# A fused five-part transformer kernel on one core: a new order of steps in a gated delta rule and its output units, and index scores computed by pairs of heads without their causally masked quarter

## What is computed

```python
idx = jnp.einsum('bqhd,bsd->bqhs', iq_c, ik)
score = jnp.einsum('bqhs,bqh->bqs', jax.nn.relu(idx), iw_c)
score = jnp.where(kpos[None, :] <= qpos[:, None], score, -jnp.inf)
sel = lax.top_k(score, k_top)[1]
```

```python
a_strict = jnp.where(strict, jnp.einsum('bhncd,bhnmd->bhncm', k_beta, k) * decay, 0.0)
sol = lax.linalg.triangular_solve(eye + a_strict, rhs, left_side=True, lower=True, unit_diagonal=True)
...
o = rmsnorm(o, out_gain).astype(proj.dtype) * jax.nn.silu(z)
...
x = x + jnp.concatenate([y_gdn, y_sc], axis=-1) @ w_mix_out[l]
```

## Time and profile before

| | us |
|---|---|
| median of 3 runs | 2455.21 |
| lowest and highest | 2454.68, 2456.13 |
| the profiled execution: its time | 2454.87 |
| its span in the trace | 2453.1 |
| TensorE busy | 2406.0 (98%) |
| VectorE busy | 1623.0 (66%) |
| ScalarE busy | 1172.2 (48%) |

### The profile page before, as it was taken

The page is one execution under the profiler, slowest core; times in us unless marked ns, Lnnn a source line. Parts: engine busy times, 40 slices in busy tenths (PEclk is TensorE's granted clock), DMA queues, the critical chain, the costliest instruction groups (busy, mean ns, idle before and its releaser), DMA issues.

```text
span 2453.1 us, 35283 instructions
## 1 busy us (share of the span) xinstructions
PE 2406.0 (98%) x14059; PEld 2075.4 (85%) x14059; DVE 1623.0 (66%) x1978; ACT 1172.2 (48%) x1406; POOL 156.7 (6%) x141
## 2 busy tenths in 40 slices
PE   7999999999999999999999999999999999999998
PEld 6888988888888888888978888888888888888887
DVE  6998886555775777596665445455877467755774
ACT  5434574544464654642554345344554334433433
POOL 1000000000200100000000000000122002200220
PEclk9999999999999999999999999999999999999999
DMA  8555546454425465554065655445565556556554
GB/s 247 190 188 172 172 138 223 140 192 144 153 84 193 146 196 175 177 166 138 3 240 172 200 183 182 155 138 172 172 202 177 204 184 193 187 190 199 178 178 147
DMA packets 337332, 422.42 MB, mean 172 GB/s; under 512 B 8478, under 2 KB 263212, under 8 KB 336700
## 3 DMA queue, kind: packets, MB, share of 16 engines
q1 hardware_dynamic: 334204, 410.87, 51.0%
q0 software_dynamic: 2544, 8.52, 1.1%
q10 hardware_dynamic: 464, 1.32, 0.2%
HBM read 418.53 MB, written 2.10 MB: 171 GB/s over the span
## 4 chain that ended last, share of the span: by engine, by line
PE 91%; DVE 5%; ACT 2%; issue 1%; DMA 0%; POOL 0%; SPq 0%; ACTq 0%; DVEq 0%
PE ps L732 35%; PE ps L733 18%; PE ps L786 10%; PE ps L788 10%; PE ps L787 10%; PE ps L1061 1%; DVE w_lo L2081 1%; ACT w_hi L1354 1%; PE ps L1053 1%; PE ps L735 1%; PE ps L736 1%; PE ps L737 1%; PE ps L979 1%; PE ps L1273 1%; PE ps L1264 1%
## 5 line engine op out<-in xcount | busy, mean ns | idle before, releaser
L732 PE MATMUL ps<-h_cat,w_hi 128*128 128x512 f32 x3840 | 1349.5, 397 | 9.8 <-DVE h_cat L2224 4.5
L733 PE MATMUL ps<-h_cat,w_lo 128*128 128x256 f32 x3840 | 1068.2, 278 | 0.0
L732 PEld LDWEIGHTS ps<-h_cat,w_hi 128*128 128x128 f32 x3840 | 720.5, 188 | 182.7 <-issue 12.2
L733 PEld LDWEIGHTS ps<-h_cat,w_lo 128*128 128x128 f32 x3840 | 722.8, 188 | 2.2 <-issue 1.9
L2081 DVE TENSOR_TENSOR w_lo<-ring,w_hi 128x2048 fp32r<-128x2048 f32 (+2 forms) x279 | 588.3, 2111 | 170.7 <-ACT w_hi L1354 168.1
L1354 ACT ACTIVATE w_hi<-ring 128x2048 fp32r<-128x2048 f32 (+2 forms) x279 | 492.6, 1767 | 94.5 <-PE ps L788 63.1
L2077 DVE TENSOR_TENSOR w_lo<-ring,w_hi 128x2048 fp32r<-128x2048 f32 (+1 forms) x136 | 302.8, 2232 | 231.1 <-ACT w_hi L1351 228.2
L1351 ACT ACTIVATE w_hi<-ring 128x2048 fp32r<-128x2048 f32 (+1 forms) x136 | 252.7, 1862 | 276.1 <-PE ps L788 254.9
L786 PE MATMUL ps<-w_hi,h_cat 128*128 128x512 f32 x640 | 250.5, 391 | 1.8 <-DVE w_lo L2077 1.8
L788 PE MATMUL ps<-w_hi,h_cat 128*128 128x512 f32 x640 | 249.2, 389 | 0.0
L787 PE MATMUL ps<-w_lo,h_cat 128*128 128x512 f32 x640 | 249.0, 389 | 0.0
(11 more groups left out here) (420 smaller groups left out, 2278.7 us busy)
## 6 DMA issues: line engine op xcount, KB each, us to landing
ring<-in_w_ffn_up SPq DMA_DIRECT2D x44, 2048.0 KB, 8.0
ring<-in_w_mix_in SPq DMA_DIRECT2D x28, 2048.0 KB, 8.3
ring<-in_even_w_in SPq DMA_DIRECT2D x27, 2048.0 KB, 8.0
ring<-in_w_ffn_down SPq DMA_DIRECT2D x16, 2048.0 KB, 8.2
ring<-in_odd_w_in SPq DMA_DIRECT2D x11, 2048.0 KB, 8.3
ring<-in_even_w_out SPq DMA_DIRECT2D x8, 2048.0 KB, 8.0
ring<-in_odd_w_out SPq DMA_DIRECT2D x8, 2048.0 KB, 8.0
ring<-in_w_mix_out SPq DMA_DIRECT2D x8, 2048.0 KB, 8.3
```

Source lines behind the costliest of these rows:

```text
L732: mm(o[:, 0:2 * T], whi[slot][:, k, :], flat(cat[:, k]), start=first, stop=False)
L733: ins = mm(o[:, T:2 * T], wlo[slot][:, k, :], cat[:, k, 0, :], start=False, stop=end)
```

## The change

1. Index scores on TensorE go by pairs of heads (2p, 2p+1), and within a pair by the 128 queries: head 2p then head 2p+1 for the first queries against keys 0 to 127 only, then both for the second queries against all 256 keys. Pairs (0, 1), (2), (3, 4), (5), (6, 7) follow units 0 to 4 of `o_gate1`. The relu and the sums work on 384 columns in place of 512; the quarter of `isum` that is now not written is set to zero once (it is masked in any case before the top-k).
2. `log_rows` of c goes ahead of `a_turn` on TensorE, and only `log_rows` of d waits for the last `g_b` tile. `attn` of a and b goes ahead of the last `post` of `g_b` on VectorE.
3. `roots_table`, a square root of one column, stands on ScalarE behind `join2_c` of b.
4. The splits of `g_out`: unit 1 goes ahead of `o_copy` of c on ScalarE and ahead of `o_total(1)` on VectorE; unit 2 goes ahead of the two `h_cat<-qkv` steps on VectorE.

```diff
@@ index scores, TensorE
-            for h in range(3 * j, min(3 * j + 3, IDX_HEADS)):
-                if h >= 6:
-                    pe.wait_ge(sem["relu_ready"], h - 5)
-                r = slice(IDX_DIM * (h % 2), IDX_DIM * (h % 2) + IDX_DIM)
+            for p in ((0, 1), (2,), (3, 4), (5,), (6, 7), (), (), ())[j]:
+                two = (2 * p, 2 * p + 1)
+                if p >= 3:
+                    pe.wait_ge(sem["relu_ready"], two[1] - 5)
                 for qt in range(TT):
-                    ins = mm(ps[2 + h % 6][:, qt * T:(qt + 1) * T], iq[r, h // 2, qt * P:(qt + 1) * P], ik[r, :],
-                             start=True, stop=True)
-                ins.then_inc(sem["idx_ready"], 1)
+                    for h in two:
+                        r = slice(IDX_DIM * (h % 2), IDX_DIM * (h % 2) + IDX_DIM)
+                        keys, c = (qt + 1) * P, qt * P
+                        ins = mm(ps[2 + h % 6][:, c:c + keys], iq[r, p, qt * P:(qt + 1) * P], ik[r, 0:keys],
+                                 start=True, stop=True)
+                        if qt == TT - 1:
+                            ins.then_inc(sem["idx_ready"], 1)
@@ relu, ScalarE
-            af(relu[:, h % 2].rearrange("p a t -> p (a t)"), ps[2 + h % 6][:], ACT.Relu).then_inc(sem["relu_ready"], 1)
+            af(relu[:, h % 2], ps[2 + h % 6][:, 0:P + T], ACT.Relu).then_inc(sem["relu_ready"], 1)
@@ log_rows, TensorE
             if t:
                 after(pe, "attn", 0, 1)
-                pe.wait_ge(sem["posted"], S["g_b"].s0 + 8)
+                if hh:
+                    pe.wait_ge(sem["posted"], S["g_b"].s0 + 8)
@@ ScalarE, the loop over its steps
+        def roots_table():
+            af(sm["sp"][:, 0:1], eps[:], ACT.Sqrt)
...
+            if (name, key) == ("join2_c", (0, 1)):
+                roots_table()
             if (name, key) == ("uw_c", (1, 1)):
                 split_to(S["g_out"].n0 + 1)
-            if (name, key) == ("o_square", (1,)):
+                after(act, "state", 0, 1)
                 split_to(S["g_out"].n0 + 2)
@@ VectorE, the loop over its steps
+        for hh in range(2):
+            go("attn", 0, hh)
...
-            if (name, key) == ("o_total", (1,)):
+            if (name, key) == ("o_gate", (0,)):
                 split_to(S["g_out"].n0 + 2)
+        split_to(S["g_out"].n0 + 3)
         for q in range(2):
...
             tt(h_lo[:, k], qkv[:, k], h_hi[:, k].bitcast(F32), ALU.subtract).then_inc(sem["h_ready"], 1)
-        split_to(S["g_out"].n0 + 3)
```

More of the change, by code:

```diff
@@ L177, in put @@
                     add(eng, name, *key)
-        put("pe", ("log_rows", a, b), ("gram", a, b), ("a_turn", a, b), ("log_rows", c, d), ("pow2", a, b),
+        put("pe", ("log_rows", a, b), ("gram", a, b), ("log_rows", c), ("a_turn", a, b), ("log_rows", d), ("pow2", a, b),
             ("gram", c), ("pow4", a), ("gram", d), ("pow4", b), ("a_turn", c), ("pow8", a), ("a_turn", d), ("pow8", b),
@@ L187, in __init__ @@
             ("join2", c, d), ("uw", c, d), ("w_state", c, d), ("o_turn", (0,)), ("o_state", c, d), ("o_turn", (1,)))
-        put("dve", ("log_diff", a, b), ("beta_decay", a, b), ("a_t", a, b), ("attn", a), ("low", a), ("attn", b), ("low", b),
+        put("dve", ("log_diff", a, b), ("beta_decay", a, b), ("a_t", a, b), ("attn", a, b), ("low", a, b),
             ("log_diff", c), ("aoff", a), ("beta_decay", c), ("log_diff", d), ("aoff", b), ("beta_decay", d), ("a_t", c),
@@ L305, in build @@
     iq = place("iq", [P, 8, T], off=AR + 24 * KB)
-    relu = place("relu", [P, 2, TT, T], off=SCR)
+    relu = place("relu", [P, 2, P + T], off=SCR)
     isum = place("isum", [P, TT, T], off=SCR + 4 * KB)
@@ L2494, in index_add @@
             for qt in range(TT):
-                w = iwt[:, qt, h:h + 1]
+                w, keys = iwt[:, qt, h:h + 1], (qt + 1) * P
+                total_, score = isum[:, qt, 0:keys], relu[:, h % 2, qt * P:qt * P + keys]
                 if h == 0:
-                    ins = nc.vector.tensor_scalar(isum[:, qt, :], relu[:, 0, qt, :], w, None, ALU.mult)
+                    ins = nc.vector.tensor_scalar(total_, score, w, None, ALU.mult)
                 else:
-                    ins = stt(isum[:, qt, :], relu[:, h % 2, qt, :], w, isum[:, qt, :], ALU.mult, ALU.add)
+                    ins = stt(total_, score, w, total_, ALU.mult, ALU.add)
             ins.then_inc(sem["idx_added"], 1)
@@ L2503, in index_beside @@
             j = 4 * i + b
+            if j == 2:
+                nc.vector.memset(isum[:, 0, P:T], 0.0)
             for h in range(3 * j - 6, min(3 * j - 3, IDX_HEADS)) if j >= 2 else ():
@@ L2782, in _ @@
         post_to(S["g_b"].n0 + 8)
-        for name, key in steps.of("dve", 18):
+        for name, key in steps.of("dve", 20):
             go(name, *key)
```

## The result

The changed kernel takes 2441.68 us (median of 5 runs, 2441.4 to 2442.31) against 2454.68 us of the kernel before (5 runs, 2453.77 to 2456.13): ratio 0.9948, 95% interval 0.9933 to 0.9962, faster by over 0.2%. The profiled execution of the changed kernel took 2442.31 us, 12.56 less than the 2454.87 of the one before.

The account below looks back on a forecast made before the run. TensorE, busy for 98% of the span, was taken as the bound. Terms 4.7 + 2.05 + 0.8 + 1.79 + 1.79 = 11.1 us; 2454.87 - 11.1 + 0.34 gives 2444.1 us, range 2442.0 to 2448.2.

Parts of the forecast that it names:

- Index scores, 4.7 us: TensorE's index blocks: pairing heads and streaming 128 columns in half the rows cuts 11.9 us to 7.15, saving 4.7.
- slot model: Index blocks on TensorE: three heads cost eight slots of 0.215 us plus 0.40 per block; slots shrink with their columns.
- bound of 2.95: Index scores: only 2.95 us saved if a slot of 128 columns costs as much as one of 256.
- rival D: Index scores: alternating halves drains the array, 0.40 us a change, making the kernel slower at 2461.9 us; chance 0.02.
- `log_rows` and `attn`, 2.05: Delta rule, second chunk's start: TensorE's waits of 1.89 and 0.16 us go, 2.05 us saved.
- The table, 0.8: ScalarE's earlier table load for roots: 0.8 us of TensorE's 1.08 wait before `w_state` of d goes.
- The output units, 1.79 + 1.79: Earlier splits on VectorE remove TensorE's two waits of 1.79 us, before `o_turn(1)` and unit 2 of g_out.
- The step that failed: Whole kernel: 11.1 us off the profiled 2454.87, plus 0.34 to the median, gives 2444.1; waits elsewhere move with their steps.
- Rival B: o_q: lighter VectorE finishes its sum in time, so the 1.51 us wait goes too, giving 2442.6 us; chance 0.04.
- Rivals A and C: A: one part falls short, 2445.9, or two, 2447.7, chance 0.22; C: later waits spend the gain, 2452 to 2455, chance 0.04.

Follow-up runs that it names:

- p11: The changed kernel with VectorE's split of unit 2 of g_out put back to its place before the change; median 2445.58 us, ratio 0.9963.
- p5: The changed kernel run again, unchanged, for the spread of its executions; five executions from 2441.06 to 2443.44 us, ratio 0.9949 to the kernel before.
- p7: The kernel before with three filler products of TensorE added in its wait ahead of g_qkv; median 2455.60 us, ratio 1.0004.
- p6: The changed kernel without the 8 filler products of TensorE between the transposes ahead of g_qkv; median 2444.18 us, ratio 0.9958.
- p10: The changed kernel with 2.5 filler products of TensorE in its remaining wait ahead of g_qkv; median 2442.00 us, ratio 0.9950.

## Why the prediction was right, and where it fell short

- **Index scores, 4.7 us: right.** 4.65 in the trace of the change, 4.7 in that of the part alone, and its two factors come out nearly as the slot model gives them. Slots of 128 columns do take half the time, so the bound of 2.95 did not apply, and rival D, alternation that drains the array, is wrong: 16 rows of alternating heads take 1.51 us. The Trainium skill, "TensorE: Matmul & The Clock Gate" (LDWEIGHTS), prices a load of 128 columns at an estimate of 107 ns. The block agrees with that only if the two halves load at the same time, as the old block already showed.
- **`log_rows` and `attn`, 2.05: right** (2.15 in the trace of the change and in that of the part alone, 2.0 by undisturbed executions). VectorE's `log_diff` of c started 2.4 us earlier, where 2.2 was forecast.
- **The table, 0.8: right** (0.8 alone, 0.8 when undone).
- **The output units, 1.79 + 1.79: right in kind, too small in size.** They measured 1.95 and 2.05. The sum took the idle time in brackets, which starts at the end of the row before:

```profile
1238.44 0.39 PE L787 MATMUL ps<-w_lo,h_cat 128*128 128x512 f32 x1
1238.67 0.39 PE L788 MATMUL ps<-w_hi,h_cat 128*128 128x512 f32 x1
1240.85 0.50 PE L786 MATMUL ps<-w_hi,h_cat 128*128 128x512 f32 x1 [1.79 <-DVE w_lo L2077]
1241.18 0.40 PE L787 MATMUL ps<-w_lo,h_cat 128*128 128x512 f32 x1
```

In a running stream of these matmuls the next starts 0.23 us behind the start of the one before (1238.44, 1238.67), and not 0.39, so 0.16 is lost beside the 1.79. The first matmul behind the wait then takes 0.50 and the next comes 0.33 later, which is 0.1 more. The forecast left both out.
- **The step that failed** is the one that set the sum against the profiled execution ("2454.87 - 11.1 + 0.34") and said that nothing else moves. The granted clock was read in two stretches, and both showed 1.00; around 820 us it was 0.50, for 1.2 us of the profiled 2454.87. The 0.34 went the same way: it led to 2455.21, the median of three executions that all lie above 2454.47, the highest of the 41 undisturbed ones. The base was thus some 1.25 us above the undisturbed level of 2453.96, while nine of the changed kernel's ten executions were undisturbed. Of the 2.4 us between the forecast of 2444.1 and the 2441.68 measured, that is 1.25; the terms were 0.5 too small (11.1 forecast, 11.6 by the same steps in the traces), and the rest of some 0.65 is left open below.
- **The larger omission is that this belongs to the change.** The waits were priced by their length. In 28 of 69 executions the kernel before reads a lower clock and takes 1.4 us more, and in every profiled execution of that kind the fall lies behind one of the waits; the changed kernel lost that time in one of ten. That is some 0.4 us on the mean of all executions, and for a single wait that comes back (p11) it is about 1.6 us on the median.
- **Rival B is wrong**: the o_q wait is still 1.51 us in the trace after. The extra came from elsewhere. **Rivals A and C are wrong**: no part fell short, and nothing was given back behind the output units.

```profile
628.97 0.47 PE L732 MATMUL ps<-h_cat,w_hi 128*128 128x512 f32 x1 [1.51 <-DVE gate L2124]
```

**What stays open.** Undisturbed executions differ by 12.2 us, while the terms by the traces make 11.6 and the single parts 11.7. The rest of some 0.6 is not shown to be an effect. Undisturbed executions of one kernel scatter by 1.2 us (before, 2453.3 to 2454.5) and 1.4 (after), and two traces of the changed kernel (its own and that of p5) move apart by up to 0.4 us at places that no edit touches. Against the undisturbed executions of their own rounds the parts make 12.2 us and the changed kernel 11.8 (p5, four executions), so the order of the two even turns round. Nor do the runs say why one kernel shows falls in 9 of 11 executions and another in 5 of 11, why filling a wait did not make them fewer (p7), or why the o_q wait of 1.51 us and the waits of 1.3 us near 468 and 1700 us never had one in 14 traces while the 1.42 ahead of g_qkv, with another 0.35 just before it, had. Idle time is thus shown to bring the clock down ahead of g_qkv (p6), and every fall seen lies behind a wait; what else has to come together is not shown.

## What to carry to other kernels

Read the clock of every execution before two are compared, and the granted clock in short windows around each wait of TensorE, not only in the long stretches: a page in tenths of full speed, in 40 slices, hides 3.4 us at half clock. A wait of TensorE was worth its length, 0.1 to 0.3 us more, and for some waits, in some executions, another 1.2 to 1.7 for the clock. So test parts of a change by their undisturbed executions or by the steps in the trace; medians of runs that mix the two made parts worth 11.7 us look like 7.8. A filler matmul in one wait gained nothing here, in either kernel (p7, p10), but fillers that are there should not be taken out as dead work (p6).

## What the hardware showed that was not expected

- TensorE's granted clock fell from 1.00 to 0.50 (2.4 to 1.2 GHz) for 3.4 us or, once (p6), for 6.8 us: ten stretches in 14 traces, all of them at one of three places, each beginning 0.04 to 1.4 us behind the end of an idle time of 1.4 to 3.8 us. Executions of the same kernel differ in it.
- Filler products change this: without eight of them ahead of g_qkv the clock fell in 5 of 5 executions, with 2.5 more in 0 of 5.
- Matmuls of 64 rows in the two halves of the array share their time even where they stand four rows apart in the program: heads 0 and 1 of the old block did. The pairs gain what the third head spent alone (1.93 us for four heads against 1.92 for three).
